# Three reorderings in a one-core transformer kernel: a head root on ScalarE, a low part on GpSimd, and the last softmax sums on TensorE

## The reference, cut to what matters

```python
def rms_norm(x, g):
    xf = x.astype(jnp.float32)
    y = xf * lax.rsqrt(jnp.mean(xf * xf, axis=-1, keepdims=True) + EPS)
    return y.astype(x.dtype) * g
...
        att = (rms_norm(heads(bq, B_HEADS), qn_g), rms_norm(heads(bk, B_KV_HEADS), kn_g), heads(bv, B_KV_HEADS))
...
        p = jax.nn.softmax(jnp.concatenate([s_loc, s_ctx, s_sink], axis=-1), axis=-1).astype(v.dtype)
...
def swiglu(h, w1, w3, w2):
    return (jax.nn.silu(h @ w1) * (h @ w3)) @ w2
```

## Time and profile before

| | us |
|---|---|
| time, median of 3 runs (1513.46 to 1514.05) | 1513.62 |
| the profiled execution's own time | 1513.86 |
| its span in the profile | 1512.1 |
| PE busy | 1479.5 (98%) |
| DVE busy | 990.7 (66%) |
| ACT busy | 706.2 (47%) |
| POOL busy | 668.1 (44%) |

### The profile page before, as it was taken

One profiled execution on the slowest core, in us unless ns is written; L12 is line 12 of the kernel. 1 busy time (PEld: TensorE's weight loads), 2 busy tenths in 40 slices (PEclk: granted clock), 3 DMA queues, 4 the chain that ended last, 5 costly groups with the idle time before them and its releaser, 6 DMA issues.

```text
span 1512.1 us, 26310 instructions
## 1 busy us (share of the span) xinstructions
PE 1479.5 (98%) x10198; PEld 1269.9 (84%) x10198; DVE 990.7 (66%) x1500; ACT 706.2 (47%) x1229; POOL 668.1 (44%) x447
## 2 busy tenths in 40 slices
PE   6999999999999999999999999999999999999997
PEld 3888874478999989999899999855569998998997
DVE  4898877579778656476667665766624655456464
ACT  4645327762733424334243444255536454445365
POOL 0031026602656334353435433355645766556473
PEclk9999999999999999999999999999999999999999
DMA  9532110045224132244546212200012314224222
GB/s 375 210 128 98 44 42 1 2 169 181 94 92 149 63 135 94 66 160 152 184 140 219 100 44 68 72 15 1 1 56 98 126 65 132 84 85 136 92 95 84
DMA packets 51674, 157.04 MB, mean 104 GB/s; under 512 B 5568, under 2 KB 13120, under 8 KB 50016
## 3 DMA queue, kind: packets, MB, share of 16 engines
q1 hardware_dynamic: 51120, 155.17, 30.1%
q0 software_dynamic: 432, 0.20, 0.1%
HBM read 153.38 MB, written 2.10 MB: 103 GB/s over the span
## 4 chain that ended last, share of the span: by engine, by line
PE 67%; DVE 4%; issue 3%; ACT 3%; POOL 2%; DVEq 0%; ACTq 0%; POOLq 0%
PE psum L3445 30%; PE psum L3472 19%; PE psum L2857 6%; PE psum L3404 3%; PE psum L3128 2%; PE psum L2933 2%; DVE product L1923 1%; PE psum L3096 1%; DVE osb L2180 1%; PE psum L3027 1%; PE psum L3417 1%; ACT fhi L1630 1%; POOL acc L1145 1%; PE psum L2956 0%; PE psum L3144 0%
## 5 line engine op out<-in xcount | busy, mean ns | idle before, releaser
L1181 POOL TENSOR_TENSOR flow<-fraw,fhi 128x512 fp32r<-128x512 f32 x168 | 233.8, 1411 | 93.0 <-ACT fhi L1630 86.4
L3472 PE MATMUL psum<-gated,fhi 128*128 128x512 f32 (+1 forms) x1032 | 253.9, 355 | 0.9 <-POOL flow L1187 0.9
L1630 ACT ACTIVATE fhi<-fraw 128x512 fp32r<-128x512 f32 (+1 forms) x272 | 163.3, 614 | 176.0 <-DMA fraw<-weights_dram 105.6
L2857 PE MATMUL psum<-act,whi 128*128 128x512 f32 (+1 forms) x1008 | 215.5, 332 | 0.1
L1187 POOL TENSOR_TENSOR flow<-fraw,fhi 128x512 fp32r<-128x512 f32 (+1 forms) x96 | 124.5, 1315 | 182.3 <-ACT fhi L1630 181.7
L3472 PEld LDWEIGHTS psum<-gated,fhi 128*128 128x128 f32 x1032 | 169.3, 188 | 29.5 <-ACT fhi L1630 1.1
L3445 PE MATMUL psum<-tlo,fhi 128*128 128x384 f32 (+1 forms) x608 | 187.9, 309 | 0.0
L3445 PE MATMUL psum<-thi,fhi 128*128 128x384 f32 (+1 forms) x608 | 187.8, 309 | 0.0
L2857 PEld LDWEIGHTS psum<-act,whi 128*128 128x128 f32 x1008 | 154.0, 189 | 20.8 <-issue 2.3
L3472 PE MATMUL psum<-gated,flow 128*128 128x512 f32 (+1 forms) x516 | 154.5, 355 | 0.0
L2563 DVE SCALAR_TENSOR_TENSOR xT<-psum,mod,xT 128x512 f32<-128x512 f32 (+1 forms) x141 | 87.6, 654 | 100.2 <-PE psum L3472 100.2
(11 more groups left out here) (291 smaller groups left out, 3339.7 us busy)
## 6 DMA issues: line engine op xcount, KB each, us to landing
fraw<-weights_dram SPq DMA_DIRECT2D x88, 512.0 KB, 3.9
adr_late<-adat_dram SPq DMA_DIRECT2D x49, 512.0 KB, 3.6
raw<-weights_dram SPq DMA_DIRECT2D x44, 512.0 KB, 3.5
fraw<-weights_dram SPq DMA_DIRECT2D x64, 256.0 KB, 2.8
adr<-adat_dram SPq DMA_DIRECT2D x26, 512.0 KB, 4.5
ada_w<-ada_dram SPq DMA_DIRECT2D x8, 1024.0 KB, 13.8
fraw<-weights_dram SPq DMA_DIRECT2D x32, 192.0 KB, 2.5
xT<-x_in_dram SPq DMA_DIRECT2D x3, 1024.0 KB, 16.8
```

The costliest lines, as they stand in the source:

```text
L1181: nc.gpsimd.tensor_tensor(low_piece(L, j, x), weight_piece(L, j, x), high_piece(L, j, x).bitcast(F32), ALU.subtract).then_inc(sem("f_lo"), 1)
L1630: A(high_piece(L, j, x)[:, 0:cols], source, ACT.Copy).then_inc(sem("f_hi"), 1)
L2857: last = MM(out_[:, o:o + t1 - t0], w_, a_[:, t0:t1], start=k == order[0] and j == 0, stop=k == order[-1] and j == 2)
L3472: last = MM(ps, w_, a_[:, t0:t1], start=k == 0 and i == 0, stop=k == nk - 1 and i == 2)
```

## The change

Three places, with no instruction added or removed.

```diff
@@ lows_of
     if PLAIN <= j < PLAIN + POOL_FORMS:
-        return lows[:1] + [("form", j - PLAIN)] + lows[1:] if j > PLAIN else lows + [("form", 0)]
+        return lows + [("form", j - PLAIN)]
@@ behind_output (scalar)
                 if n == 10:
                     linear_values(4)
-                    head_root(0)
@@ loop over the blocks (scalar)
                 if kind == "proj":
+                    if n == 10:
+                        head_root(0)
                     if L == 1 or n < 15:
                         mixer_projection(L, n, b)
@@ block_products (tensor)
-            def block_products(n):
+            def block_products(n, sums=None):
...
+                    if sums and k == 1:
+                        sums(len(U[1]) - 1)
@@ attention (tensor)
-                if L == 1:
-                    sums(len(units) - 1)
                 return sums
@@ loop over the blocks (tensor)
                 if n == FIRST[("out", 1)]:
-                    attention(1)
-                if n == FIRST[("out", 0)]:
+                    block_products(n, attention(1))
+                elif n == FIRST[("out", 0)]:
                     first_outputs(n)
```

## The result

| | before | after |
|---|---|---|
| median of the comparison, us | 1513.39 (1512.51 to 1515.06, 22 runs) | 1515.92 (1513.52 to 1522.57, 22 runs) |
| profiled execution, us | 1513.86 | 1516.94 |
| its span, us | 1512.1 | 1515.1 |

The ratio is 1.0014, 95% interval 1.0008 to 1.002. So the changed kernel is slower by about 2.1 us (0.14%), or by 2.5 if the two medians are subtracted. My sum was +1.1, and 1515.92 lies 0.3 above the upper end of my range. The verdict "within 0.2%" holds. The question is where another 1.0 to 1.4 us came from.

A forecast was written before the change was run, and what follows sets the result against it. PE was taken as the bound, busy 1479.5 of 1512.1 us. Terms -1.0 - 0.6 + 2.2 + 0.5 = +1.1 us, added to the median 1513.62, gave 1514.7 (no change); 8-in-10 range 1512.4 to 1515.6.

The forecast's parts named there:

- Part A: Block 11, near 134 us: making the head's root ahead of the projection removes PE's stall; -1.0 us.
- Part C: Near 1106 us: block 37's first tile fills PE's wait for POOL's last sums; -0.6 us, tile 7 then waits slightly.
- Part B, layer 0: POOL order in layer 0: the `flow_4_1` stall goes, but new delays eat the gain and more; +0.5 us.
- both roads: Layer 0: DVE first delays PE near 461 (0.55 us worse); form 1 first delays `xT` near 467 (about 0.35 worse).
- Part B, layer 1: POOL order in layer 1: form 1 and DVE's subtraction delay `flow_5_0`, so PE waits near 1200; +2.2 us.
- Rival 3: Layer 1: PE's idle 2.1 us lowers the clock; total passes +3.1 us, 1516.8 or more, verdict slower; chance 0.04.

The follow-up runs named there:

- e1: Kernel before with only the head's root put ahead of the projection on ScalarE; 1511.42 us against 1512.69, ratio 0.9999.
- e5: Kernel before with only POOL's form 1 moved behind weight 1 of pair 4, in layer 0 alone; 1513.05 us against 1512.31, ratio 1.0006.
- e10: The changed kernel itself measured once more, against the kernel before on the same chip; 1514.59 us against 1512.16, ratio 1.0017.
- e9: Changed kernel with DVE's last low part in layer 1 moved behind m=4; 1513.17 us against 1512.31 of the kernel before, ratio 1.001.
- e3: Kernel before with only POOL's form 1 moved behind weight 1 of pair 4, in both layers; 1516.64 us against 1512.69, ratio 1.0023.
- e6: Kernel before with only POOL's form 1 moved behind weight 1 of pair 4, in layer 1 alone; 1514.67 us against 1512.31, ratio 1.0019.
- e12: Changed kernel with three unused POOL subtractions ahead of layer 1's `flow_5_0`; 1516.74 us against 1511.98 of the kernel before, ratio 1.0033.
- e8: Changed kernel with form 1's low part behind pair 6 in both layers; 1511.40 us against 1512.16 of the kernel before, ratio 0.9996.

## Why the prediction came out as it did

- **Part A, -1.0.** Right: 1.01 at its place, and 1.3 by the medians of e1. In the profile of the result a wait for POOL's `wlo` of 1.27 us appeared near 372, and 0.6 of the gain was lost again by 395. It isn't a price of A: in the other profiles with A the wait at that place is 0.1 to 0.2, and the distance from the key turn to L varies between 259.5 and 261.4 us with it and between 260.1 and 261.0 without.
- **Part C, -0.6.** The mechanism was right (0.52, with the last tile 0.06 behind DVE), the size was right for the one execution that I had. As a forecast for the median it was too large: in three of five executions with the old order the wait is 0.2, and there C gives nothing. By these five, about -0.2 is its mean, an estimate.
- **Part B, layer 0, +0.5.** Right, with both roads seen: the wait near 461 in the profile of the result (predicted 1.5, is 1.42), the one near 467 in e5 and e10 (predicted 1.3, is 1.4).
- **Part B, layer 1, +2.2.** Right to 0.2: the stall is 1.86 of idle time, worth 2.0 from S to U, and e9 shows the mechanism. The whole chain stands 0.47 us earlier than in the earlier trace rows, by the terms ahead of it; with that, DVE's second one ends where I had it to 0.1 us, the stall is 2.02 from start to start where I had 2.14, and no refill came on top.
- **Rival 3, the clock, 0.04.** This is the step that failed. I gave it 0.04 and took it as a threshold behind which the verdict turns; it belonged into the sum as +1.6 us in about every second execution (the slower group of the result has 12 of 22 runs). It was seen in two of the four profiles that have the 1.86 us rest unfilled (result and e3; not e6 and e10), and in the one with 2.92 (e12).

With these sizes the sum is -1.0 - 0.2 + 0.5 + 2.0 + 0.5 × 1.6 = +2.1. Measured were +2.1 by the ratio, +2.5 by the medians, and +2.4 for e10. The two shares in this sum were read from a few executions after the fact, so that it comes out to the tenth is luck.

What led me wrong was how I read the witnesses. The earlier trace rows gave 0.92 over four us at the end of the program. In steps of one us the same trace of before shows where in it the fall lies:

```profile
1506.00:1507.00 1.00, 0.00 (x0) 0.00 (x0) 0.61 (x2) 0.69 (x2) 0.23 (x1) 1.00 1.04 339
1507.00:1508.00 1.00, 0.00 (x0) 0.00 (x0) 1.00 (x3) 0.00 (x0) 1.00 (x1) 0.69 1.01 338
1508.00:1509.00 1.00, 0.00 (x0) 0.00 (x0) 0.27 (x1) 0.00 (x0) 0.04 (x1) 0.50 1.04 342
```

PE does nothing from 1506 on, and the clock falls while it rests. An average over four us had made a fall to 0.50 look like a slight one. The other witness, 12 to 17 us, was none at all. PE rests there for 2.63 us (14.17 to 16.81), and the column shows 1.00. But behind the rest the matmuls run at half speed. Here are a stretch behind it, and the same step of two matmuls in it and later, all from before:

```profile
17.00:20.00 3.00, 3.00 (x8) 2.32 (x9) 3.00 (x5) 2.36 (x3) 0.00 (x0) 1.00 1.03 429
```

```profile
18.22 1.05 PE L2877 MATMUL psum<-act,whi 128*128 128x512 f32 x2
...
25.01 0.63 PE L2877 MATMUL psum<-act,whi 128*128 128x512 f32 x2
```

1.05 us is what two such matmuls take in the stretch at 0.50 behind the stall (1.06), 0.63 what they take at 1.00. Ahead of the rest PE was slow as well: eight matmuls on `ada_w` take 1.94 us at 10.40, sixteen take 2.09 at 22.19. So up to about 22 us the clock was low, the column's 1.00 is wrong there, and this rest could show neither a fall nor its absence. The one argument against rival 3 rested on it, and with it the 0.04.

## What to carry to other kernels

A stall on a busy TensorE can have a second price behind it. When a forecast makes PE idle in one piece as here (1.9 to 2.9 us), put the slow stretch into the sum with its own chance, and read the granted clock in stretches of one us around the nearest rests that the trace has. Hold the column against the duration of a step that is known at both levels; at the start of this program it shows 1.00 while PE runs at half speed. A wait seen in one execution is one sample: a second profile of the same kernel can show that half a microsecond of it is not always there to be won. And where DVE and POOL exclude each other, moving a long POOL instruction can cost more than it saves, as in layer 0 and in e8; list what DVE has ready at both places, since the one that waits goes next.

## What was not expected of the hardware

- After a rest of 1.86 us in the middle of dense work the granted clock fell to 0.50 in two executions and stayed at 1.00 in two, in the same code. After 2.92 it fell, after 0.87 it didn't. It fell about 0.6 us *after* PE was at work again (result), or just at its return (e3), and stayed low for some 3 us, which cost 1.3 to 1.6 us. The rests of 1.3 to 1.4 us near 460 or 465, in nine profiles, passed at 1.00. What decides at 1.86 us stays open.
- At the start of the program the clock is low and rises at another moment in each execution: the two matmuls of the step near 20.8 us take 1.05 us in the profile of the result and 0.62 in e10, the same kernel. The Trainium skill, "TensorE: Matmul & The Clock Gate", Part 1, says that the number of slow matmuls at the start differs between runs of one kernel; these traces agree.
- The exclusion of DVE and POOL isn't limited to DVE's subtractions: `product`, a SCALAR_TENSOR_TENSOR on two tiles, took 4.52 us instead of 1.22 behind one POOL instruction (e8).
